# Turning operands by 32-by-32 blocks and through DRAM instead of on TensorE

## The reference

```python
x = x + 0.5 * swiglu(rmsnorm(x, ffn1_norm), ffn1_w_gu, ffn1_w_down)      # "f1"
z = rmsnorm(x, mix_norm) @ w_in                                          # u, v, c_q, c_kv, k_rope, q_m, 3 gates
y_a = gelu(u) * causal_mix(layernorm(gelu(v)))                           # spatial gating
y_b = mla(c_q, c_kv, k_rope)                                             # 8 heads, low-rank queries and keys
y_c = memory_attention(q_m, mem)                                         # 4 heads of 128, 256 memory rows
x = x + (g_a*(y_a @ w_branch_a) + g_b*(y_b @ w_branch_b) + g_c*(y_c @ w_branch_c)) @ w_out
x = x + 0.5 * swiglu(rmsnorm(x, ffn2_norm), ...)                         # "f2"
# second block, conditioned: shift, scale and gate rows from silu(c) @ ada_w + ada_b
gate_b, gate_c, hv = split(modulate(rmsnorm(x)) @ conv_w_in, 3)
x = x + g1 * ((gate_b * conv3_grid(gate_c * hv, conv_w)) @ conv_w_out)   # three taps along rows of 64
x = x + g2 * swiglu(modulate(rmsnorm(x)), ...)                           # "f3"
return rmsnorm(x) * final_g
```

## Time and profile before

| what | value |
|---|---|
| median of 3 runs | 890.19 us (889.85 to 890.6) |
| the profiled execution's own time | 890.65 us |
| its span | 888.9 us |
| PE busy | 878.5 us, 99% of the span |
| DVE busy | 631.6 us, 71% |
| ACT busy | 460.7 us, 52% |
| DMA moved | 215.12 MB, mean 242 GB/s |
| chain that ended last, by engine | PE 94%, DMA 2%, DVE 1%, issue 1%, ACT 1% |

### The profile page before, as it was taken

One profiled execution on the slowest core, in us unless ns is written; L12 is line 12 of the kernel. 1 busy time (PEld: TensorE's weight loads), 2 busy tenths in 40 slices (PEclk: granted clock), 3 DMA queues, 4 the chain that ended last, 5 costly groups with the idle time before them and its releaser, 6 DMA issues.

```text
span 888.9 us, 11084 instructions
## 1 busy us (share of the span) xinstructions
PE 878.5 (99%) x4079; PEld 732.8 (82%) x4079; DVE 631.6 (71%) x883; ACT 460.7 (52%) x697; POOL 40.8 (5%) x66
## 2 busy tenths in 40 slices
PE   9999999999999999999999999999999999999996
PEld 7878888888998888888888888888888888888885
DVE  6769987837558877688578886875768766665743
ACT  6546554626688475446535554454445344444530
POOL 0010000022103000000000000001000100000000
PEclk9999999999999999999999999999999999999998
DMA  9899999774654454454699999975755577777741
GB/s 365 346 323 352 359 363 351 270 237 145 182 175 175 162 193 164 149 186 143 218 308 348 344 329 323 333 257 163 257 179 177 182 248 241 240 233 246 250 120 47
DMA packets 94879, 215.12 MB, mean 242 GB/s; under 512 B 14520, under 2 KB 46185, under 8 KB 94697
## 3 DMA queue, kind: packets, MB, share of 16 engines
q1 hardware_dynamic: 94104, 212.97, 69.8%
q10 hardware_dynamic: 720, 1.44, 0.4%
HBM read 204.66 MB, written 9.72 MB: 241 GB/s over the span
## 4 chain that ended last, share of the span: by engine, by line
PE 94%; DMA 2%; DVE 1%; issue 1%; ACT 1%; SPq 0%; POOL 0%; POOLq 0%; DVEq 0%
PE ps L741 29%; PE ps L743 29%; PE ps L742 29%; DMA t_raw<-in_f_up 2%; PE ps L679 1%; PE ps L656 1%; PE ps L649 1%; PE ps L858 1%; PE ps L874 1%; PE ps L816 0%; PE ps L850 0%; PE ps L798 0%; DVE t_wl L1209 0%; DMA t_acc<-in_xT 0%; PE ps L865 0%
## 5 line engine op out<-in xcount | busy, mean ns | idle before, releaser
L1209 DVE TENSOR_TENSOR t_wl<-t_raw,t_wh 128x1024 fp32r<-128x1024 f32 (+3 forms) x308 | 360.4, 1203 | 103.3 <-ACT t_wh L916 102.4
L916 ACT ACTIVATE t_wh<-t_raw 128x1024 fp32r<-128x1024 f32 (+3 forms) x308 | 307.8, 1040 | 106.9 <-DMA t_raw<-in_f_up 63.3
L741 PE MATMUL ps<-t_wh,t_XH 128*128 128x512 f32 (+2 forms) x640 | 250.2, 391 | 1.3 <-DVE t_wl L1209 1.3
L743 PE MATMUL ps<-t_wh,t_XL 128*128 128x512 f32 (+2 forms) x640 | 247.1, 386 | 0.0
L742 PE MATMUL ps<-t_wl,t_XH 128*128 128x512 f32 (+2 forms) x640 | 246.8, 386 | 0.0
L741 PEld LDWEIGHTS ps<-t_wh,t_XH 128*128 128x128 f32 x640 | 120.2, 188 | 24.8 <-DVE t_wl L1209 2.1
L743 PEld LDWEIGHTS ps<-t_wh,t_XL 128*128 128x128 f32 x640 | 120.1, 188 | 24.0
L742 PEld LDWEIGHTS ps<-t_wl,t_XH 128*128 128x128 f32 x640 | 120.3, 188 | 22.9
L741 PE MATMUL ps<-t_wh,t_YH 128*128 128x512 f32 x288 | 113.1, 393 | 0.2 <-DVE t_YL L1634 0.2
L743 PE MATMUL ps<-t_wh,t_YL 128*128 128x512 f32 x288 | 112.2, 390 | 0.0
L742 PE MATMUL ps<-t_wl,t_YH 128*128 128x512 f32 x288 | 112.2, 389 | 0.0
(11 more groups left out here) (225 smaller groups left out, 614.1 us busy)
## 6 DMA issues: line engine op xcount, KB each, us to landing
t_raw<-in_f_up SPq DMA_DIRECT2D x130, 512.0 KB, 5.6
t_raw<-in_f_dn SPq DMA_DIRECT2D x66, 512.0 KB, 5.5
t_raw<-in_ada SPq DMA_DIRECT2D x48, 512.0 KB, 6.3
inner_rows<-t_tp SPq DMA_DIRECT2D x60, 128.0 KB, 3.8
t_tp<-inner_rows SPq DMA_DIRECT2D x15, 512.0 KB, 5.2
t_raw<-in_mkv SPq DMA_DIRECT2D x8, 512.0 KB, 3.6
t_raw<-in_ga SPq DMA_DIRECT2D x8, 512.0 KB, 3.3
t_raw<-in_gc SPq DMA_DIRECT2D x8, 512.0 KB, 3.2
```

The costliest lines, as they stand in the source:

```text
L741: pe.matmul(o, xh, h, start=k == 0, stop=False)
L743: x = pe.matmul(o, xl, h, start=False, stop=k == n - 1)
L916: act.activation(wh[:, m % SPL, lo:w], raw[:, n % RAW, lo:w], ACT.Copy).then_inc(hi_made, 1)
L1209: dve.tensor_tensor(wl[:, n % RAW, lo:w], raw[:, n % RAW, lo:w], wh[:, m % SPL, lo:w].bitcast(F32), ALU.subtract).then_inc(drained, 1)
```

## The change

Five of the six turned operands leave PE: the memory's queries and keys, y_c, y_a, and in the convolution's first half UU and GB. They take the way of the hidden rows: `blocks` on DVE, `spill` and `reload` on SP, then copies and subtractions on ACT and DVE. There are three buffers and three scratch areas for it now (`way`: `tp`, and both halves of `acc2`), each with its own pair of semaphores. y_b and the convolution's second half stay on PE.

The list changes with it. Blocks of the keys stand beside unit 8, those of qm beside unit 12, with spill one unit and reload two units later. The memory attention's step n moves from unit 15 + 2n to 21 + 2n. The four steps for y_c begin at unit 36, those for y_a at unit 42, with the split (`y_in`) five units behind the blocks. In the convolution, the blocks of UU follow its product; spill, reload and the split (`ut_in`) stand beside units 0, 1 and 3 of gb0; the blocks of GB follow gb0; its spill and reload with the taps stand beside units 0 and 1 of cc1, the product (`gate_in`) and the split beside units 1 and 2 of hv1. The conditioning's units of `f1` begin behind unit 18 instead of 10 and end behind unit 58 instead of 57.

```diff
+        start = 18 if tag == "f1" else 10
         for i, u in enumerate(part):
             out.append(u)
-            while ada and i >= 10 and (24 - len(ada)) * 50 < (i - 9) * 24:
+            while ada and i >= start and (24 - len(ada)) * (60 - start) < (i - start + 1) * 24:
                 out.append(ada.pop(0))
...
+            8: [("blocks", "mk")], 9: [("spill", "mk")], 10: [("reload", "mk")],
+            12: [("blocks", "qm"), ("qm_stat", 0)], 13: [("spill", "qm"), ("qm_stat", 1)], 14: [("reload", "qm")], 16: [("lat_stat", "cq")], 18: [("lat_row", "cq")],
...
     for n in range(8):
-        side[15 + 2 * n] = side.get(15 + 2 * n, []) + mem(n)
+        side[21 + 2 * n] = side.get(21 + 2 * n, []) + mem(n)
+    for n, br in ((36, "c"), (42, "a")):
+        for m, step in ((0, "blocks"), (1, "spill"), (2, "reload"), (5, "y_in")):
+            side[n + m] = side.get(n + m, []) + [(step, br)]
...
-                unit("conv_cc1", m, *([("gate_turn", 0, m), ("gate_low", 0, m)] if m < 2 else []))
+                unit("conv_cc1", m, *([("spill", "gb"), ("conv_taps", 0, 0)], [("reload", "gb"), ("conv_taps", 0, 1)], [], [])[m])
...
-            unit(f"conv_hv{i}", m, ahead=5)
+            unit(f"conv_hv{i}", m, *({1: [("gate_in",)], 2: [("gate_low", 0, 0), ("gate_low", 0, 1)]}.get(i * m, [])), ahead=5)
         S.append(("conv_uu", i))
+        if i == 0:
+            S.append(("blocks", "uu"))
+            turns = [("spill", "uu")], [("reload", "uu")], [], [("ut_in",)]
...
+        if i == 0:
+            S.append(("blocks", "gb"))
...
+            def ut_in():
+                act.wait_ge(*is_back("uu"))
+                for t in (0, 1):
+                    act.activation(parts_of(uT[:, :, :].rearrange("p j (c n) -> p (j c) n", c=2), t), placed(t, "uu"),
+                                   ACT.Copy).then_inc(*ut_made.by(0, t))
...
             def mem_in_(h):
-                b, full = place["mem_in", h]
-                act.wait_ge(turned, full)
                 if h:
                     act.wait_ge(turned, place["mem_sc", h - 1][1])
-                act.activation(mqk[:, 0:256], ps[:, b, 0:256], ACT.Copy, scale=C["mqn"])
-                act.activation(mqk[:, 256:512], ps[:, b, 256:512], ACT.Copy, scale=C["mkn"]).then_inc(mqk_made, 1)
+                else:
+                    act.wait_ge(*is_back("mk"))
+                    act.wait_ge(*is_back("qm"))
+                act.activation(by_block(mqk[:, 0:256]), chunk_back(h, "qm"), ACT.Copy, scale=C["mqn"])
+                act.activation(by_block(mqk[:, 256:512]), chunk_back(h, "mk"), ACT.Copy, scale=C["mkn"]).then_inc(mqk_made, 1)
...
+            def gate_in():
+                dve.wait_ge(*taps_made.at(0, 1))
+                dve.wait_ge(*is_back("gb"))
+                for t in (0, 1):
+                    c = parts_of(cT[:, :, :].rearrange("p j (c n) -> p (j c) n", c=2), t)
+                    dve.tensor_tensor(c, placed(t, "gb"), c, ALU.mult).then_inc(*cg_made.by(0, t))
...
             def conv_uu(i):
                 if i:
-                    dve.wait_ge(turned, place["ut", 0, 1][1])
+                    dve.wait_ge(*blocked.at("uu"))
```

More of the change, by code:

```diff
@@ L484, in build @@
         drop = nc.dram_tensor("mod_rows", (48, P), F32, kind="Internal").ap()
-        inner_rows = nc.dram_tensor("inner_rows", (4, 8, 32, P), F32, kind="Internal").ap()
+        way = tp, acc2[:, 1, :], acc2[:, 0, :]
+        inner_rows = nc.dram_tensor("inner_rows", (3, 4, 8, 32, P), F32, kind="Internal").ap()
         def sem(name):
@@ L517, in build @@
         inner_keys = [(f, q) for f in FFNS for q in range(6)]
-        blocked = Signal(sem("blocked"), inner_keys)
+        turned_keys = steps("blocks")
+        blocked = Signal(sem("blocked"), turned_keys)
+        spilled, reloaded = ([sem(f"{n}{w}") for w in range(3)] for n in ("spilled", "reloaded"))
         hid_hi, hid_lo = Signal(sem("hid_hi"), both(inner_keys)), Signal(sem("hid_lo"), both(inner_keys))
-        spilled, reloaded = sem("spilled"), sem("reloaded")
         halves = steps("half")
@@ L590, in out_of, with way_of, is_back, is_out @@
                             "ukv0": "kv0", "ukv1": "kv1"}.get(name, name), t)
[L592 to L606 removed]
+        def way_of(*key):
+            return {"mk": 1, "qm": 2, "c": 1, "a": 1}.get(key[0], 0)
+        def is_back(*key):
+            w = way_of(*key)
+            mine = [k for k in turned_keys if way_of(*k) == w]
+            return reloaded[w], 16 * (mine.index(key) + 1)
+        def is_out(*key):
+            w = way_of(*key)
+            mine = [k for k in turned_keys if way_of(*k) == w]
+            return spilled[w], 64 * (mine.index(key) + 1)
+        def way_width(*key):
+            return 512 if key[0] in FFNS and key[1] == 5 else 1024
+        def placed(t, *key):
+            rows = way[way_of(*key)][:, 0:way_width(*key)]
+            return rows.rearrange("p (i t c n) -> p t c i n", i=4, t=2, n=32)[:, t]
+        def chunk_back(c, *key):
+            return way[way_of(*key)].rearrange("p (i t c n) -> p c t i n", i=4, t=2, n=32)[:, c]
+        def parts_of(a, t):
+            return a[:, :, t * P:t * P + P].rearrange("p c (i n) -> p c i n", i=4)
+        def inner_chunks(a, q):
+            return a[:, 4 * q:min(4 * q + 4, 22), :]
+        def by_block(rows):
+            return rows.rearrange("p (t i n) -> p t i n", t=2, i=4)
         def psum_2(bank):
@@ L1331, in hid, with blocks @@
                                                  op1=ALU.mult).then_inc(*hid_made.by(f, g, t))
-            def blocks(f, q):
-                n = inner_width(q) // 2
-                dve.wait_ge(*hid_made.at(f, 2 * q + (q < 5), 1))
-                dve.transpose(tp[:, 0:2 * n].rearrange("p (t n) -> p t n", t=2), hp[:, :, 0:n]).then_inc(*blocked.by(f, q))
+            def blocks(what, *key):
+                to = way[way_of(what, *key)]
+                if what in FFNS:
+                    q, = key
+                    n = way_width(what, q) // 2
+                    dve.wait_ge(*hid_made.at(what, 2 * q + (q < 5), 1))
+                    dve.transpose(to[:, 0:2 * n].rearrange("p (t n) -> p t n", t=2), hp[:, :, 0:n]).then_inc(*blocked.by(what, q))
+                    return
+                if what == "mk":
+                    dve.wait_ge(mk_made, 2)
+                    rows = MK
+                elif what == "qm":
+                    dve.wait_ge(*evac.at("qm", 1))
+                    rows = QM
+                elif what == "c":
+                    dve.wait_ge(mval, 8)
+                    rows = QM
+                elif what == "a":
+                    dve.wait_ge(ya_made, 2)
+                    rows = U
+                elif what == "uu":
+                    dve.wait_ge(*uu_made.at(0, 1))
+                    rows = UU
+                else:
+                    dve.wait_ge(*gb_made.at(0, 1))
+                    rows = GB
+                for t in (0, 1):
+                    m = dve.transpose(to[:, 512 * t:512 * t + 512].rearrange("p (j c n) -> p c j n", j=4, c=4),
+                                      rows[:, t, :].rearrange("p (c j n) -> p c j n", c=4, j=4))
+                m.then_inc(*blocked.by(what, *key))
@@ L1558, in att_val @@
                 if h == 0:
-                    dve.wait_ge(turned, place["y", "a", 1][1])
+                    dve.wait_ge(*blocked.at("a"))
                 dve.wait_ge(turned, full)
```

94 lines of the change are left out of this document (45 added, 49 removed), and 4 rows, old and new, of the table side.

## The result

The changed kernel takes 904.94 us (median of 4 runs, 903.86 to 907.45), against 890.33 for the kernel before beside it: ratio 1.0169, 95% interval 1.0146 to 1.0192. I had forecast 895.6 and a range of 886 to 900: slower was right, the size was not. The span of the profiled execution is 902.1 us, 13.2 longer.

A forecast was written before the change was run, and what follows sets the result against it. PE, busy 99% of the span, was taken as the bound. Transposes -5.2, conditioning -1.3, middle +7.7, convolution +2.5 and clock +1.7 gave +5.4 on 890.65: 896.05, or 895.6 as a median; range 886 to 900.

The forecast's parts named there:

- The failed step: In f1, fewer conditioning fetches issued at every unit before the last, so no weight would come later than before.
- The gain that I named: In f1, later conditioning would remove PE's two waits for low parts of weights: -1.3 us, bounds 0 and -1.6.
- The middle's wait: Memory attention beside V and latent queries: PE waits for ACT's evacuations up to ukv1, +7.7 us, bounds +6.0 and +10.5.
- the clock's term: Behind the middle's wait the granted clock falls once, to half speed: +1.7 us, bounds 0 and 3.4.
- the chain: ACT's and DVE's steps in order from the first scores' start T, behind unit 23, letting ukv1 start at T+20.35.
- The drain: Rival: each ACT table load between Exp and Gelu holds ACT longer than the row's 1.28 us: 899.4 us; chance 0.04.
- The convolution: Second UU ready at t0 + 35.3, PE asks at t0 + 32.75: +2.5 us, bounds 0 and 3.1.
- The transposes: 48 transposes leave PE (memory attention, y_c, y_a, UU, GB) at 0.109 us each: -5.2 us.
- What I costed at nothing: Keys and qm, y_a, y_c have enough cover; DVE's 7.5 us of block turns and SP's 24 spills cost nothing.
- Rival 1: Evacuations of V, uq0, uq1 and the second UU come before PE asks: -6.5 us, 883.7 us; chance 0.22.

The follow-up runs named there:

- b18slow: Kernel before with the conditioning of f1 begun behind unit 18 at the rate of before (24 in 50 units): 889.67 us, ratio 0.9987.
- s18 runs: Five kernels with f1's conditioning behind unit 18 at the old rate and the mended convolution, differing in which other parts of the change they keep: ratios 0.9961 to 0.9989.
- a10 runs: Changed kernel with f1's conditioning back behind unit 10, alone or with further edits to the middle or convolution: ratios 1.0018 to 1.0091.
- a10: Changed kernel with only the conditioning of f1 set back behind unit 10: 899.38 us, ratio 1.0085.
- a10_keep: Changed kernel with f1's conditioning back behind unit 10, plus 8, 18 and 28 identity transposes on PE ahead of uq1, ukv0 and ukv1: 899.19 us, ratio 1.0091.
- a10_m17_gate: Changed kernel with conditioning back behind unit 10, memory attention beside 17 + 2n, and the gate's product and split behind the second UU: 893.88 us, ratio 1.0029.
- s18_conv_g2: Kernel before with conditioning behind unit 18 at the old rate, UU and GB through DRAM, UU's spill earlier, gate's split behind second UU: 887.71 us, ratio 0.9961.
- s18_nomem_g2: Changed kernel with conditioning behind unit 18 at the old rate, mended convolution, memory's turns on PE, y_c and y_a through DRAM: 888.67 us, ratio 0.9975.
- b18_spill1: Kernel before with the change's f1 conditioning start and rate, and f1's hidden-row spills, reloads and splits one unit later: 891.45 us, ratio 1.0005.

## Why the prediction was wrong

- **The failed step** is "At every unit before the last, fewer conditioning fetches have been issued than before, so nothing comes later." It cost the forecast 6.9 us: -1.3 predicted, +5.6 measured. The count up to a unit says nothing, because the ring of ten is full early, with or without the conditioning (between 20 and 35 us SP stands 12.4 us for a buffer that PE still holds, before as after), and what isn't fetched then can't be saved for later. What counts is the rate from there on: 24 in 42 units in place of 24 in 50. And I priced the queue as if only memory were behind it, while SP, in order, stands at every spill until DVE has turned the blocks. The gain that I named does exist at the old rate: the six traces with the later start at that rate (b18slow and the s18 runs) have f1 at -1.4 to -0.4, the seven with the start of before (before and the a10 runs) at 0 to +1.9, 2.0 apart in the mean.
- **The middle's wait** was right as a mechanism and in its place, and somewhat small: 9.4 with the clock's term, 11.4 measured. ukv1 started 1.05 us later than the chain said; the rest lies behind it, up to bra0, where PE also waits 0.8 us for Exp in the latent attention, which I hadn't followed. The drain that the Trainium skill, "ScalarE: Activation LUTs" (What ACT_TABLE_LOAD costs), adds to a load does not show here either: the next activation starts 1.29 to 1.30 behind the start of a load where nothing else holds it.
- **The clock's fall** came, to half of full speed, twice in the middle where I had counted one. The Trainium skill, "TensorE: Matmul & The Clock Gate" (HAM oscillation — how this bites in real kernels), has the work behind an idle gap start cold. In a10's trace it does, from the first product of ukv0 at 263.48; in that of the change the first six products there still run at full speed, 0.23 us apart, and the fall comes after them. My term for it failed all the same: a10_keep took the fall away and the time stayed. The term's size came from the warming transposes; they take 0.23 us each where later ones add 0.109, but the trace gives a granted clock of 1.00 over them, so whether they show the lower clock is open. In the middle the wait and the clock must not be added, since other engines set the pace there up to bra0; behind co's wait in a10_m17_gate they do add.
- **The convolution** was right in kind, 2.5 predicted, 1.5 measured: the way through DRAM took 10.2 (647.30 to 657.52) where I took 11.2, and the queue behind it was 0.5 shorter. By that chain 1.0 remains, and the wait for UU is 1.1; the other 0.4 of the cost I haven't traced.
- **The transposes** gave what I had for them where nothing new waits: 1.9 us for 16 in the mended convolution, where I had 1.75.
- **What I costed at nothing** held for y_a at bra0 and for the first head's copies, where PE waits for neither. It did not hold for the block turns on DVE: y_c and y_a bring waits for Exp into the latent attention, +0.5 us to bra0 between s18_conv_g2 and s18_nomem_g2 where 16 transposes should have given -1.75. That DVE's free share would cover them was read from the average.
- **The sum**: 6.9 for f1 and 2.0 for the middle less 1.0 for the convolution make 7.9 of the 9.3 us between forecast and median. The rest is, to a tenth, how far the profiled executions, from which these are read, lie from the medians: 1.1 below it after, 0.46 above it before.
- Rival 1, no new wait, is refuted for the change as it stands. For the convolution it can be had by order alone; the memory attention beside 17 + 2n still makes PE wait 1.9 us at ukv0.

What stays open is whether the ring or the memory would bind at the denser rate, if SP never stood at a spill: b18_spill1 is within the uncertainty of no change, and its trace still shows 2.2 us of waits for low parts. From 60 to 120 us DVE is busy for 59.3 of 60 us there and the DMA engines for a share of 0.98, so DVE could bind as well as the memory.

## What to carry to other kernels

Before work is moved off the bounding engine, follow the chain that the result must take on the other engines, in their own order, and ask at each evacuation whether the next product is behind it: of 5.2 us saved, only the 1.9 of the convolution were kept, where the order could be mended. An in-order DMA queue that also carries stores is held by whatever the stores wait for; a ring only covers that up to its length, and a slightly denser stream of fetches (here 24 in 42 units instead of 50) can uncover it. Where other engines set the pace up to the next meeting point, a better clock or a shorter wait on one engine can be given back there, as between the first scores and bra0 here; so ask who is late at that point before adding the two up.

## Not expected of the hardware

ACT's table loads cost 1.28 us each and no more, even back to back with an Exp between them (256.08 and 258.59). The granted clock fell to 0.50 behind waits of PE of 2.25 and 3.22 us in the middle, and 54 transposes of the identity in those waits kept it at 1.00.
